# Modulation products in four 32-column groups of the array in turn, and operand buffers at multiples of 512 bytes, in a fused transformer block

## What is computed

```python
mx = jnp.split((sc @ w_mod[l] + b_mod[l])[:, None, :], N_MOD, axis=-1)   # sc = silu(c), 6 rows of 1024
mc = jnp.split((scc @ w_mod[l] + b_mod[l])[:, None, :], N_MOD, axis=-1)  # scc = silu(c_ctx)
px = split_proj(modulate(x, pre_mix_g[l], mx[0], mx[1]) @ w_in[l])
pc = split_proj(modulate(xc, pre_mix_g[l], mc[0], mc[1]) @ w_in[l])
oc, s_f, s_b = hgrn_bidir(*hgrn_inputs(pc, lb_f, lb_b), zero_state, zero_state)
ox, _, _ = hgrn_bidir(*hgrn_inputs(px, lb_f, lb_b), s_f, s_b)
mix_x = mixer_output(ox, px, rows, w_out[l], ...)
x = x + mx[2] * rms_norm(mix_x, post_mix_g[l])
hx = swiglu(modulate(x, pre_ffn_g[l], mx[3], mx[4]), ffn_w_gate[l], ffn_w_up[l], ffn_w_down[l])
x = x + mx[5] * rms_norm(hx, post_ffn_g[l])
```

## The kernel before

| product | weights | moving data |
|---|---|---|
| input projection | `ring` (128) | `hT` (96) |
| output projection | `catS` (96) | `split` (128) for two of eight k, `woA` (96) for six |
| gate and up | `split` (128) for the first tile of a round, `more` (96) for the second | `h2Ta`, `h2Tb` (96) |
| down | `mid` (96) | `more`, `slotX` (96); in the last round `split` (128) |

## Time and profile before

### The profile page before, as it was taken

The page is one execution under the profiler, slowest core; times in us unless marked ns, Lnnn a source line. Parts: engine busy times, 40 slices in busy tenths (PEclk is TensorE's granted clock), DMA queues, the critical chain, the costliest instruction groups (busy, mean ns, idle before and its releaser), DMA issues.

```text
span 1560.8 us, 17854 instructions
## 1 busy us (share of the span) xinstructions
PE 1461.7 (94%) x6789; PEld 1147.9 (74%) x6789; DVE 742.3 (48%) x1026; ACT 375.4 (24%) x561; POOL 356.2 (23%) x151
## 2 busy tenths in 40 slices
PE   7699999999999877986998999999999999999995
PEld 1488888888888723435877888888888888888884
DVE  1802387688688798238552231332313323132237
ACT  2521321322131242235342211111111211112113
POOL 1421111111011074202133321222212221222114
PEclk9799999999999987988999999999999999999998
DMA  9110100100000153403221211111111101111022
GB/s 357 50 41 27 41 28 28 41 27 27 27 27 27 55 201 101 156 14 126 91 81 54 81 41 41 55 54 45 36 54 54 54 28 52 54 54 44 23 109 108
DMA packets 92655, 101.93 MB, mean 65 GB/s; under 512 B 3118, under 2 KB 77091, under 8 KB 92610
## 3 DMA queue, kind: packets, MB, share of 16 engines
q1 hardware_dynamic: 92610, 101.32, 19.8%
HBM read 92.92 MB, written 8.39 MB: 65 GB/s over the span
## 4 chain that ended last, share of the span: by engine, by line
PE 81%; DVE 10%; issue 5%; POOL 2%; ACT 2%; DMA 1%; DVEq 0%; POOLq 0%; SPq 0%; ACTq 0%
PE bank L515 79%; DVE conv_sum L1299 2%; DVE Q L1369 1%; DVE S L1401 1%; POOL xres L1195 1%; DVE xfull L1266 1%; DVE part L1319 1%; DVE K L1361 1%; DVE h2f L1557 1%; DVE catS L1488 0%; DVE cat L1507 0%; DMA mask<-masks 0%; PE bank L742 0%; PE bank L628 0%; POOL h2Tb L1129 0%
## 5 line engine op out<-in xcount | busy, mean ns | idle before, releaser
L515 PE MATMUL bank<-hT,ring 128*128 128x512 f32 (+1 forms) x1632 | 365.6, 381 | 2.1 <-POOL hT L1129 1.6
L515 PEld LDWEIGHTS bank<-hT,ring 128*128 128x128 f32 x1632 | 287.7, 190 | 61.1 <-POOL hT L1129 1.8
L1129 POOL TENSOR_TENSOR ring<-ring_in,ring 128x1024 fp32r<-128x1024 f32 x28 | 69.5, 2482 | 402.6 <-ACT ring L838 402.6
L1602 DVE TENSOR_TENSOR y<-bank,y 128x512 f32<-128x512 f32 x160 | 109.9, 690 | 86.8 <-PE bank L515 86.4
L1129 POOL TENSOR_TENSOR more<-raw,more 128x1024 fp32r<-128x1024 f32 x32 | 76.5, 2406 | 312.6 <-ACT more L1056 170.2
L1580 DVE TENSOR_TENSOR mid<-bank,sgm 128x512 f32<-128x512 f32 x44 | 30.4, 692 | 225.9 <-ACT sgm L1080 225.9
L515 PE MATMUL bank<-slotX,mid 128*128 128x512 f32 x480 | 134.8, 389 | 0.0
L515 PE MATMUL bank<-more,mid 128*128 128x512 f32 x480 | 134.8, 389 | 0.0
L515 PE MATMUL bank<-h2Tb,split 128*128 128x512 f32 x528 | 127.5, 401 | 4.3 <-POOL h2Tb L1129 4.3
L515 PE MATMUL bank<-h2Ta,split 128*128 128x512 f32 x528 | 125.0, 396 | 1.2 <-POOL split L1129 1.2
L515 PEld LDWEIGHTS bank<-h2Tb,split 128*128 128x128 f32 x528 | 100.9, 191 | 29.0 <-issue 4.5
(11 more groups left out here) (169 smaller groups left out, 1645.5 us busy)
## 6 DMA issues: line engine op xcount, KB each, us to landing
mraw<-in_w_mod SPq DMA_DIRECT2D x48, 512.0 KB, 6.6
ring_in<-in_w_in SPq DMA_DIRECT2D x28, 512.0 KB, 3.8
raw<-in_ffn_w_gate SPq DMA_DIRECT2D x22, 512.0 KB, 3.8
raw<-in_ffn_w_up SPq DMA_DIRECT2D x22, 512.0 KB, 3.8
raw<-in_ffn_w_down SPq DMA_DIRECT2D x22, 512.0 KB, 3.3
xst<-in_x SPq DMA_DIRECT2D x8, 512.0 KB, 12.4
raw<-in_w_out SPq DMA_DIRECT2D x8, 512.0 KB, 4.8
x1t<-in_x SPq DMA_DIRECT2D x8, 512.0 KB, 3.3
```

The source lines that it names most:

```text
L515: return pe.matmul(o, l, r, start=start, stop=stop, skip_group_check=True)
L1129: return pool.tensor_tensor(lo, full, hi.bitcast(F32), ALU.subtract)
L1602: ins = dve.tensor_tensor(y[:, t, sl], bank[4 + i % 4][:], y[:, t, sl], ALU.add)
```

## The change

Modulation: `silc` gets 32 columns for each k, of which 30 are zero, so that a product fills a group of 32 columns of the array and 32 partitions of PSUM. The four products of an even and an odd step k go to partitions 0, 32, 64 and 96 of one bank, so even and odd k accumulate apart. ScalarE copies the whole bank in one instruction (128x512 for two of 2x512). Instead of the eight transposes, eight products with the 128x128 pieces of `mrow` as weights and two columns of `sel` as moving data turn the rows and add even and odd k; `sel[:, q, :]` is made of the identity matrix by VectorE and picks rows 32q and 64+32q. One more memset clears `silc`.

Addresses: the place of `raw` and that of `hT` are rounded up to multiples of 512 bytes. With that `raw`, `split`, `ring`, `ident`, `vT`, `hT`, `cat` and all that is placed relative to them lie at 0 modulo 512; `silc` and `sel` at 384, `ones` at 160. `split`, `ring` and `more` become two or three tensors each at the same relative places as before.

```diff
         RAW = 3
+        def align(to):
+
+            free[0] = (free[0] + to - 1) // to * to
+
+        def slots(name, places, dt=F32R):
+
+            return [sb(f"{name}{'abcdef'[i]}", [P, 2, DM], dt, offset=o) for i, o in enumerate(places)]
+
+        align(512)
+        RAW0 = free[0]
         raw = sb("raw", [P, RAW, DM])
-        split = sb("split", [P, 2, 2, DM], F32R)
-
-        ring = sb("ring", [P, RAW, 2, DM], F32R, offset=spot["raw"])
-        ring_in = sb("ring_in", [P, RAW, 2, DM], offset=spot["raw"])
+        split = slots("split", [RAW0 + 12288, RAW0 + 20480])
+        RING = [RAW0, RAW0 + 8192, RAW0 + 16384]
+        ring = slots("ring", RING)
+        ring_in = slots("ringin", RING, F32)
+        free[0] = RAW0 + 28672
...
-        silc = sb("silc", [P, KT, 2])
+        silc = sb("silc", [P, KT, 32])
+        sel = sb("sel", [P, 2, 2])
...
+        align(512)
         hT = sb("hT", [P, 2, KT, TOK], F32R)
...
-        mrow = sb("mrow", [P, 2, DM], offset=A0 + 32768)
+        mrow = sb("mrow", [P, 2, BANK], offset=A0 + 32768)
...
                     for q in range(2):
-                        ins = mm(bank[b0 + q][0:2, :], silc[:, k, :], (mraw if n < 2 else mraw2)[:, k, q * BANK:(q + 1) * BANK],
-                                 k == 0, k == KT - 1)
+                        g = 32 * (2 * (k % 2) + q)
+                        ins = mm(bank[b0][g:g + 32, :], silc[:, k, :], (mraw if n < 2 else mraw2)[:, k, q * BANK:(q + 1) * BANK],
+                                 k < 2, k >= KT - 2)
...
                         c0 = (n % 4) * 2 * KT + 2 * j
-                        ins = pe.transpose(bank[bt][:, c0:c0 + 2], mrow[0:2, n % 2, j * P:(j + 1) * P], ident[0:2, 0:2])
+                        ins = mm(bank[bt][:, c0:c0 + 2], mrow[:, n % 2, (j % 4) * P:(j % 4 + 1) * P], sel[:, j // 4, :], True, True)
...
-                for q in range(2):
-                    ins = act.activation(mrow[0:2, n % 2, q * BANK:(q + 1) * BANK], bank[b0 + q][0:2, :], ACT.Copy)
-                ins.then_inc(mod_row, 1)
+                act.activation(mrow[:, n % 2, :], bank[b0][:], ACT.Copy).then_inc(mod_row, 1)
...
             step(dve.memset(eps[:], EPS))
+            step(dve.memset(silc[:], 0.0))
...
+            for q in range(2):
+                dve.tensor_tensor(sel[:, q, :], ident[:, 32 * q:32 * q + 2], ident[:, 64 + 32 * q:66 + 32 * q], ALU.add)
+            dve.tensor_tensor(silc[:, :, 0:2].rearrange("p k a -> p a k"), silt[:],
                               vec[:, 0:2 * KT].rearrange("p (a k) -> p a k", a=2), ALU.mult).then_inc(cols_done, 1)
```

More of the change, by code:

```diff
@@ L200, in kernel_program @@
         mraw = sb("mraw", [P, KT, DM], offset=spot["cat"])
-        mrow = sb("mrow", [P, 2, DM], offset=A0 + 32768)
+        mrow = sb("mrow", [P, 2, BANK], offset=A0 + 32768)
         mraw2 = sb("mraw2", [P, KT, DM], offset=A0)
-        vT = sb("vT", [P, 2, BANK], offset=spot["raw"] + RAW * 2 * DM * 4)
+        vT = sb("vT", [P, 2, BANK], offset=RAW0 + RAW * 2 * DM * 4)
         part7 = sb("part7", [P, SEQ], offset=A0 + 40960)
@@ L224, in kernel_program @@
         mid = sb("mid", [P, 2, 2, 2, SEQ], F32R, offset=W0)
-        more = sb("more", [P, 3, 2, DM], F32R, offset=W0 + 32768)
+        more = slots("more", [W0 + 32768, W0 + 40960, W0 + 49152])
         mid32 = sb("mid32", [P, 2, BANK], offset=W0 + 57344)
@@ L230, in wo_part @@
         def wo_part(q, k):
-            return split[:, k, q] if k < 2 else woA[:, k - 2, q]
+            return split[k][:, q] if k < 2 else woA[:, k - 2, q]
         WO_AT = [2, 3, OUT_AT]
@@ L243, in ffn_part @@
         def ffn_part(q, j):
-            return split[:, j, q] if j < 2 else (more[:, j - 2, q] if j < 5 else slotX[:, q])
+            return split[j][:, q] if j < 2 else (more[j - 2][:, q] if j < 5 else slotX[:, q])
         bank = [es.enter_context(nc.psum_tensor(f"bank{i}", [P, BANK], F32)) for i in range(8)]
@@ L422, in load_tile @@
                     sp.wait_ge(gemm_full, s * NUNIT + (last_unit(mine[-1]) + 1 - NUNIT))
-                sp.dma_start(ring_in[:, SLOT[p], 1, :].rearrange("p (k n) -> p k n", k=KT),
+                sp.dma_start(ring_in[SLOT[p]][:, 1, :].rearrange("p (k n) -> p k n", k=KT),
                              win[:, :, bass.ds(col, P)]).then_inc(raw_in[SLOT[p]], 16)
@@ L584, in w @@
                 def w(k):
-                    return [ring[:, SLOT[p], q, k * P:(k + 1) * P] for q in range(2)]
+                    return [ring[SLOT[p]][:, q, k * P:(k + 1) * P] for q in range(2)]
                 if kind == "vt":
@@ L837, in head_hi @@
                 act.wait_ge(raw_in[SLOT[p]], head_fill(s, p) * 16)
-                act.activation(ring[:, SLOT[p], 0], ring_in[:, SLOT[p], 1], ACT.Copy).then_inc(w_hi, 1)
+                act.activation(ring[SLOT[p]][:, 0], ring_in[SLOT[p]][:, 1], ACT.Copy).then_inc(w_hi, 1)
             mod_rows(0)
@@ L1132, in head_lo @@
                 pool.wait_ge(w_hi, s * NTILE + (p + 1))
-                lo_part(ring[:, SLOT[p], 1], ring_in[:, SLOT[p], 1], ring[:, SLOT[p], 0]).then_inc(w_lo, 1)
+                lo_part(ring[SLOT[p]][:, 1], ring_in[SLOT[p]][:, 1], ring[SLOT[p]][:, 0]).then_inc(w_lo, 1)
             for p in range(2):
@@ L1216, in _ @@
                               ALU.subtract).then_inc(cols_done, 1)
-            dve.tensor_tensor(silc[:].rearrange("p k a -> p a k"), silt[:],
+            for q in range(2):
+                dve.tensor_tensor(sel[:, q, :], ident[:, 32 * q:32 * q + 2], ident[:, 64 + 32 * q:66 + 32 * q], ALU.add)
+            dve.tensor_tensor(silc[:, :, 0:2].rearrange("p k a -> p a k"), silt[:],
                               vec[:, 0:2 * KT].rearrange("p (a k) -> p a k", a=2), ALU.mult).then_inc(cols_done, 1)
```

## The result

The changed kernel takes 1525.52 us, the median of four runs (1524.49 to 1530.73), beside 1563.68 for the kernel before on the same chip: a ratio of 0.9767, interval 0.974 to 0.9795. The profiled span is 1522.7.

What follows compares the result with a forecast made beforehand. TensorE was taken to bound the kernel, with 81% of the chain that ended last. 1560.8-14.4-7.7-4.8 = 1533.9 us for the span, 2.6 more for the median: 1536.5; own range 1526 to 1547, stated range 1478 to 1557.

Steps and rivals of the forecast that it cites:

- Addresses: 512-column matmuls with `split` or `ring`: 226.7 ns instead of 233, 2208 on the chain at 6.6 ns, 14.4 us taken.
- The groups: Modulation steps in the last head: 4.6 us from single steps, copy and turnings, 3.1 in the tail, together 7.7.
- middle of two bounds: Modulation records: one runs beside the first of the next matmul only; a lone step takes 3 record times, not 4.
- The lower bound, a quarter: Modulation records: everything of four groups at once, a quarter of the present 0.43 us a record.
- Rival D: Modulation steps: all groups overlap fully, up to another record time less a step, some 8 us together; 1528 us, chance 0.05.
- The start: Second modulation pass: last block lands at 34.7 us, first `xfull` at 39.3 instead of 44.12, 4.8 us less.
- the queue is already full: Transfers in the start: issuing the second pass's blocks earlier gains nothing.
- The clock (F): Start: shorter bursts leave TensorE at 1.2 GHz through the second pass, gain 0.5 not 4.8; 1541 us, inside the forecast's 0.42.
- rival A: All aligned 512-column products: an absolute place costs too, 12.1 ns each, -53.8 us more; 1482.7 us, chance 0.25.
- A with D: Both rivals together, 512-column products and modulation groups: 1478 us, taken as the lower end of the stated range.

Runs made afterwards that it cites:

- experiment 1: The changed kernel with the old modulation, so only the places differ from the kernel before: 1550.09 us, 0.9901 of before.
- Experiment 3: The changed kernel with weights (and one moving buffer) moved off 0 modulo 512 bytes, in two sets of places: 1547.96 and 1532.53 us, one run each.
- experiment 2: The changed kernel with the old addresses (128 and 96 modulo 512), so only the modulation differs from before: 1543.43 us, 0.9848 of before.
- Experiment 4: The changed kernel with 128 bytes added ahead of `raw` and of `hT`, both operands at 128 modulo 512: 1526.66 us in one run.

## Why the prediction was right, and where it was too small

**Addresses.** Forecast 14.4 us, measured 15.1 by the medians and 14.2 by the spans (experiment 1). By stretch, in the changed kernel: the heads 7.1 forecast (312 and 756 matmuls) and 7.7 measured, the output projection 0.5 and 0.7, gate and up 7.0 and 6.3. The 6.6 ns each and the count of matmuls on the chain were right, within 0.7 us a stretch. The rule it was put down to, the same place modulo 512 bytes, was right for this change and too narrow: 256 is the period. One small loss was not counted: products of 256 columns with `ring`, spaced 118.3 ns on average before (difference 32), take 119.5 now (difference 0), and 114.4 at difference 64. With 288 in the heads that is 0.3 us.

The rule of the Trainium skill that speaks against the change (SBUF — State Buffer, Who interferes with whom: TensorE reads through two independent ports and waits for no one) doesn't settle this case. Experiment 3 moved the weights alone, by 32 bytes, and the spacing went from 226.7 to 233.2 ns: the two reads are not independent in time. Whether TensorE ever waits for another engine's reads no run here asks.

**The groups, the step that failed.** "Starts are in order, and the two records of one matmul use the same group, so a record can run beside the first of the next matmul, no more" was the middle of two bounds, taken without a row for it, and it was wrong: starts are not in order across groups, each group has its own line. The lower bound, a quarter, holds as far as the groups are filled: a lone step has two, and the row of five has 6 of its 20 records in the busiest. A lone step saves 0.83 us, not 0.43; 20 records take 2.77 us, not 4.7. With that, the last head's sum is 16 x 0.83 + 0.3 - 2.6 + 8.74 - 2.77 + 0.5 - 1.3 = 16.2 for 7.7, and 16.7 was measured. Rival D named this mechanism; its "some 8 us" beside the forecast was close, at 9.

The Trainium skill's figure for three column tiles (TensorE: Matmul & The Clock Gate, Part 3), 2.38 times, was the better guide than my middle: 8.77 to 2.77 is 3.2 times with four groups and the tail counted. The same page's Part 2 says that matmuls stay in program order and only weight loads are pulled ahead. Here the first record of a later step started 0.446 us before the last of the one ahead of it.

**The start.** Forecast 4.8, measured 6.7. The chain behind the last block was right: 4.6 us forecast from its landing to the first `xfull` (34.7 to 39.3), 4.4 measured (33.1 to 37.5), and 4.4 again in experiment 2 (34.1 to 38.5). What the sum held fixed and the runs did not is the landing, and 1.6 of the missing 1.9 us are that. It doesn't hang on when TensorE frees the places. With the old steps the last block is issued almost 4 us later than in the changed kernel, and it landed at 32.7, earlier still. With the new steps and the early issue, but the old addresses, it landed at 34.1. The tile `mraw` there, places only and then groups only:

```profile
L424 SPq DMA_DIRECT2D mraw<-in_w_mod x1: 328/328/328, 25.6 to 25.6; - x1
...
DMA to landing us min/median/max: 7.1/7.1/7.1
```

```profile
L427 SPq DMA_DIRECT2D mraw<-in_w_mod x2: 429/430/430, 21.4 to 21.8; - x2
...
DMA to landing us min/median/max: 11.5/11.9/12.3
```

So "the queue is already full" was right: from the first landing to the last the DMA share is 1.04 or 1.05 in the kernel before, the changed one, places only and groups only. What changed is the rate, and it goes with the addresses that the transfers write to:

| place of `mraw` modulo 512 bytes | kernels | second pass's blocks land apart, us | first to last landing, us |
|---|---|---|---|
| 96 or 128 | before, experiments 2 and 4 | 1.28 in each | 25.3 to 25.6 |
| 0 | changed, all other experiments | 1.23 to 1.25 | 24.2 to 24.6 |

Experiment 4 differs from the changed kernel in the addresses alone. Its first `xfull` came at 38.9 for 37.5, and its last block at 34.5 for 33.1: 0.9 us by the rate, 0.5 by a later first block. In the changed kernel 1.2 of the 1.6 us are this, a gain of the places that the prediction did not have; the other 0.4 is the first block, which landed anywhere from 8.3 to 9.3 us in the twelve kernels, and is luck. The table rests on one profiled execution of each kernel, and no run asks which other places are as good as 0. The turning took 1.95 us, as its nearest row had it.

**The clock (F).** Its condition came in part. TensorE's granted clock fell to half from 20.4 to 27.3 us, behind three lone steps with waits of 0.2 to 0.4 us ahead of them and in the middle of the turning, where the kernel before had it in full from 13.9 to 48 us:

```profile
20.40:27.30 6.90, 4.54 (x19) 2.10 (x20) 3.84 (x6) 4.78 (x7) 4.31 (x2) 0.51 1.04 416
27.30:37.50 10.20, 8.68 (x50) 3.33 (x44) 1.04 (x3) 1.93 (x4) 0.81 (x1) 1.00 1.03 421
```

The first steps of the second pass ran under it, and it cost nothing: each still started within 0.05 us of its block's landing. From 27.3 to 37.5 us the clock was full. The next falls stand in the stretch that VectorE paces.

**The sum.** 14.4 + 7.7 + 4.8 = 26.9 forecast; 14.8 + 16.7 + 6.7 = 38.2 measured, 38.1 by the spans. Of the 11.3 us between, 9.0 are the one assumption on the groups, 1.9 the start (1.2 of it the quicker transfers, 0.4 luck), 0.4 the matmuls' addresses. The time lay inside the stated range because that range had been drawn wide for rival A, which wants a spacing of 214 to 216 ns; all stayed at 226.7. The range's lower end was also mis-added: A with D is 1482.7 - 8 = 1475, not 1478.

## What to carry to other kernels

Place the two operands of a matmul at the same offset modulo 256 bytes of a partition: it cost nothing and gave 6.6 ns of 233 on each float32r matmul of 512 columns (those of 256 columns lost 1.2 ns). Multiples of 512 bytes, which this change happened to take, also made the transfers into them some 2% quicker (1.25 us a block of 512 KB for 1.28), which counts where the queue is full. Products with a few weight columns belong in different 32-column groups; two suffice for a pair, and the gain is nearly a full factor per group in use, as long as the row of products is long and the groups are evenly filled (20 records: 8.77, 4.49 and 2.77 us with one, two and four). Before making a filler cheaper, look whether it could stand in a wait: here, in the last head, the order alone was worth as much as the groups.

## What the runs showed that was not expected

- The price of a mismatch is nearly flat, 5.8 to 7.3 ns whatever the difference, but only 2.4 at 192.
- In experiment 3, `slotX` and `mid` both lie at 0, and yet three matmuls of `slotX` and three of `morec` (at +192) in turn start 1.39 us apart for six, 231.7 ns each; the `slotX` pairs alone average 229.8. So a product also pays for its neighbour's place. That fits a clash between one product's moving data and the weight load of the next, but no run took the two apart.
- For 256 columns difference 64 was the cheapest of the three seen (114.4 ns, against 118.3 at 32 and 119.5 at 0). Why the order is another than for 512 columns stays open, as does what the 13.3 ns are that 226.7 has over 512/2.4 = 213.3.
